# The chunked recurrence as a software pipeline over token blocks

## The reference, cut to what matters

```python
def _rwkv7_step(S, inp):
    r, w, k, v, kk, b = inp
    sa = jnp.einsum('bhvk,bhk->bhv', S, kk)
    S = S * w[:, :, None, :] - sa[..., None] * b[:, :, None, :] + v[..., None] * k[:, :, None, :]
    return S, jnp.einsum('bhvk,bhk->bhv', S, r)
```

## Time and profile before

| | |
|---|---|
| Median of 3 runs | 4870.73 us (4864.91 to 4880.74) |
| Profiled execution, its span | 4866.1 us |
| `rwkv_core`, first layer: up to its first level / from there to its end | 29.8 us / 452.6 us |
| `rwkv_core`, second layer: the same | 30.8 us / 443.2 us |
| PE busy over the whole span | 87% |
| DVE, ACT, POOL busy | 57%, 32%, 30% |

### The profile page before, as it was taken

How to read it: one execution, slowest core, us unless ns; L and a number is a source line. 1 busy time by engine, 2 the same in 40 slices (tenths; PEclk the granted TensorE clock), 3 DMA queues, 4 the chain that set the end, 5 groups by cost and what they waited for, 6 DMA issues and landing times. The chain is left out here.

```text
span 4866.1 us, 103654 instructions
## 1 busy us (share of the span) xinstructions
PE 4241.5 (87%) x43026; PEld 3280.6 (67%) x43026; DVE 2749.5 (57%) x4666; ACT 1537.1 (32%) x2721; POOL 1475.8 (30%) x1090
## 2 busy tenths in 40 slices
PE   6999889877998799989986998689788988978898
PEld 4887688854667587778884666578545677854566
DVE  3465444455666447544445665665575656557565
ACT  1332222223552123222222553210155421015542
POOL 2232233302013323233331111565232135523213
PEclk8999999988999899989998999789899999989999
DMA  6455532342135445642324133533403253340325
GB/s 194 146 186 189 145 78 59 81 159 83 42 83 178 148 153 198 197 122 71 78 59 148 45 92 112 172 99 106 149 7 81 67 183 124 104 142 17 81 53 181
DMA packets 517941, 561.41 MB, mean 115 GB/s; under 512 B 112732, under 2 KB 412284, under 8 KB 515380
## 3 DMA queue, kind: packets, MB, share of 16 engines
q1 hardware_dynamic: 389876, 475.93, 31.6%
q10 hardware_dynamic: 127616, 78.95, 5.6%
HBM read 366.75 MB, written 192.23 MB: 115 GB/s over the span
## 5 line engine op out<-in xcount | busy, mean ns | idle before, releaser
L1096 PE MATMUL pr_acc<-hH,pr_wh 128*128 128x512 f32 (+1 forms) x1288 | 482.4, 375 | 0.0
L1097 PE MATMUL pr_acc<-hL,pr_wh 128*128 128x512 f32 (+1 forms) x1288 | 466.0, 362 | 0.0
L1098 PE MATMUL pr_acc<-hH,pr_wl 128*128 128x512 f32 (+1 forms) x1288 | 465.6, 361 | 0.0
L2586 ACT ACTIVATE an_p<-an_p,an_stat 128x1280 f32<-128x1280 f32 (+5 forms) x372 | 339.7, 914 | 162.8 <-DVE an_stat L2664 157.2
L2033 POOL TENSOR_TENSOR rk_ml<-rk_lmask,rk_g 128x384 f32<-128x384 f32 x240 | 232.1, 999 | 464.1 <-DVE rk_g L1963 464.1
L2526 PE MATMUL an_t<-ident,an_p 128*128 128x128 f32 x2152 | 319.5, 283 | 40.3 <-ACT an_pT L2593 27.8
L2619 POOL TENSOR_TENSOR an_kl<-an_k,an_kh 128x1280 fp32r<-128x1280 f32 (+3 forms) x36 | 78.5, 2179 | 898.5 <-DVE an_qh L2644 898.5
L2526 PEld LDWEIGHTS an_t<-ident,an_p 128*128 128x128 f32 x2152 | 236.7, 142 | 163.9 <-issue 68.0
L2660 DVE CUSTOM_DVE_ANT_0 an_p<-an_s,an_mask 128x256 f32<-128x256 f32 (+8 forms) x308 | 274.9, 892 | 101.7 <-PE an_s L2509 68.4
L1971 DVE TENSOR_TENSOR rk_tu<-rk_tu,rk_ps 128x512 f32<-128x512 f32 x300 | 190.3, 634 | 237.0 <-PE rk_ps L1796 237.0
L1465 POOL TENSOR_TENSOR sp_sl<-sp_w,sp_sh 128x512 fp32r<-128x512 f32 x172 | 246.0, 1437 | 196.8 <-DVE sp_sh L1540 178.4
(11 more groups left out here) (382 smaller groups left out, 10181.1 us busy)
## 6 DMA issues: line engine op xcount, KB each, us to landing
CHK<-ri_out SPq DMA_DIRECT2D x24, 1920.0 KB, 8.1
rk_in<-CHK SPq DMA_DIRECT2D x120, 384.0 KB, 5.9
pr_w<-in_w_in ACTq DMA_DIRECT2D x58, 512.0 KB, 4.1
UT<-pr_out SPq DMA_DIRECT2D x45, 640.0 KB, 4.6
sp_w<-in_w_in ACTq DMA_DIRECT2D x50, 512.0 KB, 5.2
U<-sp_c SPq DMA_DIRECT2D x100, 256.0 KB, 2.0
mod_w<-in_w_mod SPq DMA_DIRECT2D x16, 1024.0 KB, 8.0
mo_w<-in_w_out SPq DMA_DIRECT2D x16, 1024.0 KB, 9.6
```

The lines of the kernel that those rows point to most:

```text
L1096: nc.tensor.matmul(out, wh[:, u, k, 0:m], hi, start=(k == 0), stop=False)
L1097: nc.tensor.matmul(out, wh[:, u, k, 0:m], lo, start=False, stop=False)
L1098: ins = nc.tensor.matmul(out, wl[:, u, k, 0:m], hi, start=False, stop=(k == KT - 1))
L2586: nc.scalar.activation(row, row, ACT.Exp, bias=stat[:, n % NPM, j, 1:2], scale=heads[groups[n][0]].scale, accum_out=total[:, n % 4, j:j + ...
```

## The change

Only `rwkv_core` changes. What each step computes stays the same; where its operands lie and when it runs changes.

1. **Tiles.** TU now holds, for each chunk c, the straight half U on `half[c]` and the transposed half T on the other partitions, and D's output has one bank for each chunk (banks 4 and 5). `level_w` runs on the tiles (1, 0) and (0, 1). In `level_d` the transposed products run on (0, 1) and (1, 0) and the straight ones on (0, 0) and (1, 1). D now fills both banks, so it waits for DVE's subtraction of the group just before. `start_t` computes both halves, with 16 products instead of 8, and ACT copies 512 columns instead of 256. `grams` computes with 24 products instead of 16: 16 of 64 columns and 8 of 128.
2. **Order.** PE's stream becomes the following, in the notation above. S is solve, O outputs, G grams, R state, T turned, s start_t, b bv. Round brackets are jobs of the block before, square ones of the next block.

```diff
-        def level_w(b, u, lv, g):
...
-            pe.wait_ge(aw.sem, aw.nth(NW * b + k - 1))
+            after(pe, aw, k - 1)
             for q in range(4):
                 d, h = q // 2, q % 2
                 for c in range(2):
-                    ins = nc.tensor.matmul(wbank(u, k)[half[c], q * CH:(q + 1) * CH], ML[half[c], u, g, d, h, lv, :],
-                                           TU[half[c], u, g, q, 0, :], start=True, stop=True)
+                    far = half[1 - c]
+                    ins = nc.tensor.matmul(w_bank[k % 2][half[c], q * CH:(q + 1) * CH], ML[far, u, g, d, h, lv - 1, :],
+                                           TU[far, u, g, c, q, :], start=True, stop=True)
...
+        def level_d(b, lv, g):
+            u, k = b % 2, number(b, lv, g)
+            pe.wait_ge(aw.sem, aw.nth(k + 1))
+            after(pe, dl, k)
             for q in range(4):
+                if lv < NL:
                     for c in range(2):
-                        nc.tensor.matmul(o[half[c], q, 0, :], TU[half[c], u, g, q, 1, :], Ws[half[c], g, q, :],
+                        nc.tensor.matmul(d_at[half[1 - c], c, q, :], TU[half[c], u, g, c, q, :], Ws[half[c], g, q, :],
                                          start=True, stop=True)
                 for c in range(2):
-                    ins = nc.tensor.matmul(o[half[c], q, 1, :], Ws[half[c], g, q, :], TU[half[c], u, g, q, 1, :],
+                    ins = nc.tensor.matmul(d_at[half[c], c, q, :], Ws[half[c], g, q, :], TU[half[c], u, g, c, q, :],
                                            start=True, stop=True)
             ins.then_inc(pd.sem, 1)
...
+        def level(b, lv, g):
+            k = number(b, lv, g)
+            dve.wait_ge(pd.sem, pd.nth(k + 1))
+            if lv < NL:
+                o = TU[:, b % 2, g, :, :, :]
+                nc.vector.tensor_tensor(o, o, d_at, ALU.subtract).then_inc(dl.sem, 1)
+            else:
+                for c in range(2):
+                    o = TU[half[c], b % 2, g, c, :, :]
+                    ins = nc.vector.tensor_tensor(o, o, d_at[half[c], c, :, :], ALU.subtract)
+                ins.then_inc(dl.sem, 1)
```

More of the change, by code:

```diff
@@ L1705, in _ @@
[L1705 to L1709, removed]
+                sp.dma_start(ec[:], T["EC"].rearrange("g p d c -> p g d c")).then_inc(cst.sem, 16)
+                load(1)
+                for b in range(NB):
+                    if b and b + 1 < NB:
+                        sp.wait_ge(pt.sem, pt.nth(NP * b))
+                        load(b + 1)
+                    receptances(b)
+                    if b:
+                        store(b - 1)
@@ L1714, in _ @@
             def _(pe):
-                warm(core, bank[0][:, 0:256])
+                warm(core, bank[2][:, 0:256])
                 pe.wait_ge(zero.sem, zero.nth(2))
                 pe.wait_ge(cst.sem, cst.after(1))
-                def grams(b, u, g):
-                    pe.wait_ge(dl_in[g].on(u), dl_in[g].step(b, u))
-                    pe.wait_ge(dg.sem, dg.nth(2 * NP * b + 2 * g))
-                    for d in range(2):
[L1724 to L1730, removed]
+                tiles = [(c, h) for c in range(2) for h in range(2)]
@@ new lines, in grams @@
+                def grams(b, g):
+                    u = b % 2
+                    pe.wait_ge(d_in[g].on(u), d_in[g].step(b, u))
+                    if g:
+                        pe.wait_ge(dm.sem, dm.nth(NP * b + g))
+                    elif b >= 2:
+                        pe.wait_ge(dq.sem, dq.nth(NP * (b - 2) + 2))
+                    else:
+                        after(pe, ab, NP * b)
+                        after(pe, au, NP * b)
+                    if g == 2 and b >= 2:
+                        pe.wait_ge(dh.sem, dh.nth(2 * (b - 1)))
+                        pe.wait_ge(dy.sem, dy.nth(2 * (b - 1)))
+                    for d in range(2):
+                        for x, arr, a0, n in ((0, A_BH, A_KT, 1), (1, A_BH, A_RT, 1), (2, A_KH, A_KT, 2)):
+                            for c, h in tiles:
+                                rows, tok = half[h], half[c]
+                                o = gram_at[g][h][half[1 - c if x == 0 else c], d * 256 + x * CH:d * 256 + (x + n) * CH]
+                                ins = nc.tensor.matmul(o, D[rows, u, g, d, arr, tok], D[rows, u, g, d, a0:a0 + n, tok], start=True, stop=True)
@@ new lines, in _ @@
+                for b in range(NB):
+                    for g in range(NP):
+                        starts(b, g)
+                        levels(b, g)
+                    if b:
+                        diagonals(b - 1)
+                diagonals(NB - 1)
+    n = NP * NB
+    spent([(x, NB) for x in d_in] + [(v_in, NB), (rt_in, NB), (stored, NB), (zero, 2), (cst, 1), (dgp, NB)]
+          + [(x, n) for x in (pg, dm, u_ok, half_u, ml, pt, ax, pu, au, pb, ab, px, at_x, pq, dq)]
+          + [(x, PER * NB) for x in (pw, aw, pd, dl)] + [(x, 2 * NB) for x in (pn, py, dh, dy)])
```

615 lines of the change are left out of this document (348 added, 267 removed).

## The result

The changed kernel takes 4915.0 us (median of 4 runs, 4899.1 to 4924.8), the kernel before 4869.4 beside it: ratio 1.0081, 95% interval 1.0059 to 1.0102. It is slower by 0.8%, some 40 us by the ratio (the two medians lie 46 us apart); the forecast was 4826, faster, with 4880 as its upper bound. The profiled execution spans 4923.0 us.

The account below looks back on a forecast made before the run. PE was taken to be bound by its instruction supply, 3.77 us per 256 instructions. Per layer 413.8 supply + 8 late waits + 4 last jobs = 425.8 against 447.9 us, giving 4826 us in all, range 4755 to 4880.

Parts of the forecast that it names:

- The block of 256 instructions: PE's instruction stream: arrives in blocks of 256 instructions (128 matmuls with their weight loads), one ahead at most.
- 3.77 us: PE's instruction supply: mean time to replace one block of 256 instructions, read from four restarts in outputs.
- B: Rival for level_d: D gains nothing from four tiles, 1.2 us per block lost, 4848 us; chance 0.12.
- The count: Instruction fetches in the first layer from its first level on: 103 before, 109.75 after the added products.
- A: Rival for the whole function: instruction supply doesn't bind and execution decides, 4632 us; chance 0.08.
- the tiles' faster D: D in levels 1 to 4 on four tiles: execution minus 5.6 us per block, mostly hidden behind instruction supply.
- Levels 1 to 3: First three levels of a block: instruction supply sets their time, 8.5, 11.3 and 8.5 us.
- The start: Start of each layer: constants later, U sooner; taken as 0, bounds minus 5 and plus 5 us per layer.
- Supply: Instruction fetches from the first level on: 109.75 at 3.77 us each, 413.8 us per layer.
- rival C: Rival for fetches during loads: they queue behind the load and get slower, 4.09 us each, 4897 us; chance 0.18.
- the break-even of 3.97: Mean time per instruction fetch, in us, from which the changed kernel would be slower than before.
- Waits: D waiting for DVE's subtraction: 34 us per block, covered by 42; late waits charged 0.8 per block, 8 per layer.

Follow-up runs that it names:

- number 1: Changed kernel with four more unused 2-column products in each level_w, 0.94 of a fetch more per block: 4986.5 us, ratio 1.0228.
- (11): Changed kernel with 32 of the 64 columns in every product of W and D, same instructions and loads: 4930.6 us, ratio 1.0113.
- number 12: The kernel of number 9, but D waits for the subtraction just before it, not the one before that: 4877.6 us, ratio 1.001.
- number 9: Changed kernel's order and buffers with the products of the kernel before, D on two tiles in two banks in turn: 4849.3 us, ratio 0.9943.
- number 5: Kernel before the change with loads of 8 of 128 partitions from block 2 on: 4841.1 us, ratio 0.9936.
- (13): The kernel of number 9 with 48 more unused 2-column products per block, 0.75 of a fetch: 4897.0 us, ratio 1.0052.
- number 2: Changed kernel with loads of 8 of 128 partitions from block 2 on: 4872.2 us, ratio 0.9997.

## Why the prediction was wrong

*What held.* The block of 256 instructions and, away from the load, nearly its 3.77 us (3.66 above, 3.86 at the mean; number 1). Four tiles at 14.6 ns, so that B fell. The count: 109.75 fetches forecast, 111 seen, 363 - 348 = 15 in all. That supply and not execution decides (11), so that A fell. That the tiles' faster D is mostly not cashed. Levels 1 to 3 to 0.1 us in block 5, to 1.2 at the mean of the blocks. The start: 32.3 for 29.8 us, inside plus or minus 5. The Trainium skill's buffer of 2048 instructions for PE ("Runtime: NRT & Kernel Launch", section "Instruction fetch mechanics"), kept as rival A, has no sign in these traces: PE still stops after 127 or 128 matmuls.

*What failed first: the 3.77 us were put on all fetches ("Supply").* I had timed restarts at a DMA share of 0.01 and 0.02 only. In the two stretches under the load they are 5.5 and 5.9 us apart. By the starts of the transfers in blocks 1 to 8 of both layers, the intervals in which data fill under a tenth of the DMA engines last 3.86 us at the mean, those over half 5.30. This is rival C in its mechanism, a fetch held up by a load, and nearly in its price: it said 4.09 us and 4897; the changed kernel's mean pitch is 467.5 / 111 = 4.21 us in the first layer, and the break-even of 3.97 is crossed. But C's title, that fetching gets slower than before, is not what happened: the kernel before has the same delays, 3.97 and 5.94 us, and a mean pitch of 452.6 / 103 = 4.39. Thin loads put the cost at 41 us, 20 per layer. C got 0.18 because PE "keeps its pace with loads running, 90% busy"; that busy share was an average over the function, while the load takes 10 us of a block. Rows of exactly that stretch of the kernel before would have shown it.

*What failed second: the single buffer ("Waits").* I summed the circle D, subtraction, D over a block, found 34 us under 42, and charged 8 us per layer for what was late. The runs give 33 us, 16 per layer. The charge of 0.8 us per block is about right for blocks 1 to 8 (0.8 and 0.5 above). What failed is that I worked the circle out for a block in the middle, where other jobs part the D's, and took it for all ten: in block 0 and block 9 those jobs are missing, and most of the wait lies there. Its cost is above the idle time booked on it, 16 us per layer by the medians for 9.9 in number 12, but an error of 7 and a part of up to 6 us for the clock lie over that difference, and the profile lists neither waits under 0.15 us nor what a wait takes from the overlap of matmuls. PE might also ask for the next block of instructions only once it has come some way into the present one, so that a wait postpones the fetch as well; the later starts of the transfers (1.79 for 1.71 us at the mean) would agree. None of these was isolated.

*What both rest on: the gain was mis-sized.* The forecast amounts to 447.9 us, minus 60 us of before that 103 x 3.77 = 388 doesn't cover, plus 25 for the fetches, plus 12. Those 60 were taken as gaps that the new order closes. The order closed 14 per layer (number 9). Another 15 was traffic (number 5), which no order of PE's jobs removes. The price of the added products was right: 25 per layer forecast, 27 measured (13). So the change bought 0.75 of a fetch and a wait, 43 us per layer, for an order worth 14 and a last step worth 9, of which the tiles have at most all.

Of the 40 us per layer between 425.8 and 465.9, 36 lie in blocks 1 to 8 (375.7 us for 8 x 42.5) and 4 in the rest. Of the 36, traffic accounts for 18 (number 2) and the pitch away from the load, 3.86 for 3.77 over 88.5 fetches, for 8; some 10 are not apportioned. That the single buffer's cost in blocks 0 and 9 doesn't show as more than 4 means that the forecast had too much for something else there, and which term is open. Some 18 us of the span's difference of 57 lie in stages that the change doesn't touch, in this one pair of executions. Four tiles with two D buffers were not tried.

## What to carry to other kernels

Where PE runs many small products, count its instructions before its columns: here 256 of them cost 3.3 to 4 us with hardly any work in them, and tiles that run at double rate while adding products cost more than they gave. Time a repeating stall once beside an idle DMA queue and once under the load, and give the load its place. Work out a circle of waits for the first and the last block too, where the jobs that part its steps in the middle are missing. Here a second buffer was worth 33 us, while the step to four tiles gained 19 and cost that buffer.

## What the hardware showed that I had not expected

- While a load fills the DMA engines for 10 us (283 GB/s at a share of 1.08), some 16 KB instruction fetches, about two per block, start 1 to 2 us later. Taking most of the load's bytes out gained 41, 31 and 26 us in three kernels. The transfer itself hardly lengthens: mean 1.10 us in the changed kernel and 1.11 with thin loads.
- With half the columns in the products of W and D the granted clock of `rwkv_core` was 0.91 in both layers, for 0.95 and 0.96 in the changed kernel, so more of it ran at 1.2 GHz (windows of number 11), though the steady blocks took the same time:

```profile
559.93:1067.72 507.79, 385.42 (x14180) 358.09 (x14181) 210.16 (x404) 132.76 (x331) 160.91 (x220) 0.91 0.29 75
2143.10:2648.18 505.08, 386.11 (x14180) 359.22 (x14181) 210.18 (x404) 132.62 (x331) 161.00 (x220) 0.91 0.29 75
```
